# Where the rows of the moving operands stand in SBUF: from a stagger of 16 bytes to one fixed distance from the weights

## The chip, the cores and the metric

The kernel runs on one core of a Trainium2 chip. The metric is the device time of the one launch, in microseconds (us); lower is better. The same inputs are used for both kernels, and both compute the same values with the same instructions.

## The reference

Two transformer blocks follow each other, each with two layers, on 256 tokens of width 1024. Everything heavy is a matrix product of the 256 tokens with a weight matrix:

```
h = h + 0.5 * swiglu(rmsnorm(h, ffn1_norm[i]), ffn1_w_gu[i], ffn1_w_down[i])   # block 1, D_FF = 2816
u = rmsnorm(h, mix_norm[i])
... = jnp.split(u @ w_in[i], ...)            # conv branch, latent attention, two gates
h = h + merged @ w_o[i]
h = h + 0.5 * swiglu(rmsnorm(h, ffn2_norm[i]), ffn2_w_gu[i], ffn2_w_down[i])
gate = jax.nn.sigmoid(rmsnorm(h, ple_norm[i]) @ w_ple_gate[i])
h = h + gate * (p[i] @ w_ple_proj[i])

a = rmsnorm_2(h, norm_mix_pre[i])            # block 2, D_FF_2 = 4096
u = jnp.einsum('bsd,de->bse', a, w_in[i])    # sparse attention, convolution, pooling
h = h + rmsnorm_2(mix @ w_out[i], norm_mix_post[i])
m = jnp.square(jax.nn.relu(m @ w_up[i])) @ w_down[i]
h = h + rmsnorm_2(m, norm_mlp_post[i])
gate = jax.nn.sigmoid(h @ ple_gate[i])
h = h + gate * (p[i] @ ple_proj[i])
```

All of it is float32.

## The kernel before

Activations lie transposed: the 128 partitions hold 128 of the 1024 features, a row along the free dimension holds the 256 tokens (1024 bytes) of one block of features, and eight rows (k = 0 to 7) hold the whole state. Each float32 operand is split into a high part, rounded to the format `float32r`, and a low part, the rest. A product of two operands is three matmuls, weights high by x high, weights high by x low, weights low by x high, into one PSUM bank. `product` writes them, at L2028, L2029 and L2030. In nearly all of them the stationary operand is a tile of 128 x 128 of the weights, loaded anew for each matmul by a weight load (PEld), and the moving operand is a row of 256 tokens.

Weights come in chunks of 128 x 2048 (one MB) by DMA into `raw` (three buffers), ScalarE rounds a chunk into `w_hi` (L800) and VectorE subtracts it into `w_lo` (L1313), in rings of four. Within a chunk a weight tile starts at a multiple of 512 bytes.

The order of the work is written out by hand for each engine in one program of four parts (block 1 twice, block 2 twice), with semaphores between the engines. The kinds of matmuls that matter here are:

- `project`, `pair` and `halves`: eight rows of `xh` and `xl` against a chunk of weights, m = 0 and 1, 48 matmuls a chunk, into `work`. In timelines: `work<-xh,w_hi`, `work<-xl,w_hi`, `work<-xh,w_lo`. Four calls of `accumulate` in each layer of block 2 read `xh` and `xl` as well, into `acc`.
- `accumulate`: two rows of the inner tile `hh` and `hl` (in the arena `ra`) against a chunk of the down projection, 48 matmuls, into `acc`. In timelines `acc<-ra,w_hi` and `acc<-ra,w_lo`. There are 76 such chunks: 11 in each of the four feed-forward nets of block 1, 16 in each of the two of block 2. The output projection of the latent attention also goes through it, with rows `oh` and `ol`: 4 chunks in each of two layers.
- the gate: eight rows `gh` and `gl` (also in `ra`) against the gate weights, 16 chunks, 48 matmuls each.
- the projection `w_o` (`work<-ra`): eight rows `mh` and `ml` in `ra`, 8 chunks.
- by token in block 2: the rows of `xh` and `xl` are the stationary operand there, and the weights move (`work<-w_hi,xh`).

The addresses: in the built program `w_hi` starts at byte 25728 of a partition, `w_lo` at 58496, `xh` at 99456, `xl` at 107776 and `ra` at 188288. All of these but `xl` are 128 modulo 256, so counted from the weights' own address modulo 256 they are at 0, and `xl` at 128. The constant `ROW = T + 4` puts the rows of `xh`, `xl`, `hh`, `hl`, `gh` and `gl` 1040 bytes apart. So row k of `xh` and of `gh` is 16k bytes past the weights' own address modulo 256 (0 to 112), and row k of `xl` and of `gl` 128 + 16k (128 to 240). The inner tile has four rows r of each part, 16r for the high part and 64 + 16r for the low part. Below, this number is called the distance of a row. The rows `mh`, `ml`, `oh` and `ol` are 1024 bytes apart, and all of them have distance 0. In the index scores of block 2 (`dots`, `acc<-ka,ra` and `acc<-kb,ra`) the stationary operand is a tile in `ra` at 128 modulo 256 and the keys, high and low, start at 0 modulo 256 (`ka` is at byte 137984, `kb` at 144128), so there every moving row stands at distance 128 from its stationary tile.

Of the kernel before, what the change touches and what calls it, by code (L numbers as in the profile page):

```python
# [34 lines left out]
F32R = mybir.dt.float32r  # L35
# [5 lines left out]
P = 128  # L41
T = 256
TB = T // P
D = 1024
KD = D // P
# [10 lines left out]
CH = 2048  # L56
WORK = 4

ROW = T + 4
EPS = 1e-6  # L60
LN_EPS = 1e-5
NEG = -1e30
# [235 lines left out]
def build(nc, ins, out):  # L298
    with ExitStack() as ctx:
        def sb(name, shape, dt=F32):  # L300
            return ctx.enter_context(nc.sbuf_tensor(name, shape, dt))
# [6 lines left out]
        w_hi = sb("w_hi", [P, RING, CH], F32R)  # L308
        w_lo = sb("w_lo", [P, RING, CH], F32R)
        h = sb("h", [P, KD, T])  # L310
        xh = sb("xh", [P, KD, ROW], F32R)[:, :, 0:T]
        xl = sb("xl", [P, KD, ROW], F32R)[:, :, 0:T]
        consts = sb("consts", [P, C_KEPT])
        rot_r = sb("rot_r", [P, 2, P], F32R)
        zero_r = sb("zero_r", [P, P], F32R)
# [14 lines left out]
        ra = sb("ra", [P, 10240], F32R)  # L330

        def cut(arena, at, *dims):
            n = 1
            for d in dims:
                n *= d
            v = arena[:, at:at + n]
            if len(dims) == 2:
                v = v.rearrange("p (a b) -> p a b", a=dims[0])
            if len(dims) == 3:
                v = v.rearrange("p (a b c) -> p a b c", a=dims[0], b=dims[1])  # L340
            return v

        ident = consts[:, C_ID:C_ID + P]
        ones = consts[:, C_ONES:C_ONES + P]
        mask1 = consts[:, C_MASK:C_MASK + 384]
# [3 lines left out]
        lneps_col = consts[:, C_COL + 3:C_COL + 4]  # L349

        gs, si, us, hid = (cut(fa, i * 1024, 2, 2, T) for i in range(4))
        hh, hl = (cut(ra, i * 4 * ROW, 2, 2, ROW)[:, :, :, 0:T] for i in range(2))
        sq = cut(fa, 4096, KD, T)

        lat = cut(fa, 0, 6, T)
# [23 lines left out]
        krph, krpl = ra[:, 7680:7936], ra[:, 7936:8192]  # L379
        mh, ml = cut(ra, 0, KD, T), cut(ra, 2048, KD, T)  # L380

        gh, gl = (cut(ra, 4 * ROW * 4 + i * KD * ROW, KD, ROW)[:, :, 0:T] for i in range(2))

        pp = cut(fa, 0, KD, T)
        gate = cut(fa, 2048, 4, 2, T)
# [2276 lines left out]
```

## Time and profile before

| | before |
|---|---|
| median of 3 runs | 1977.84 us |
| lowest and highest | 1977.26 and 1979.76 us |
| span of the profiled execution | 1978.2 us |
| TensorE matmul busy | 1935.2 us, 98%, 16060 matmuls |
| TensorE weight load busy | 1916.9 us, 97% |
| VectorE busy | 1350.9 us, 68% |
| ScalarE busy | 996.9 us, 50% |
| GpSimd busy | 237.4 us, 12% |

No time of the profiled execution is given beside its span, 1978.2 us; the span is 0.4 us over the median of the other runs, so there is nothing around it to be added.

A matmul's own duration in the profile (280 ns) is longer than the time from its start to the next one's (about 118 ns), since matmuls are pipelined and their ends are modelled. What a matmul costs is read from starts: take the start of the first and of the one behind the last of a run of matmuls, and divide by their number. The timeline shows starts to 10 ns, so a run of 24 or 48 is exact to 0.4 ns a matmul or better, a group of three only to some 3 ns.

### The profile page before, as it was taken

The numbers are of one execution on the slowest core, as the hardware profiler recorded it, in microseconds if no ns is written. First come the engines' busy times: TensorE is split into PE (matmuls) and PEld (weight loads), VectorE is DVE, ScalarE is ACT, GpSimd is POOL, SyncE is SP. The second block draws the span as 40 slices with busy tenths as digits, with TensorE's granted clock in tenths as the row PEclk, the third lists the DMA queues.
The fourth block names the chain that finished last, engine by engine and source line by source line (L and its number), as shares of the span: only waits on it lengthen the run. The fifth ranks groups of instructions, "written<-read, shape, count | busy, mean of one in ns | idle before, by whom it ended". The sixth has DMA issues, their size and how long they took to land.

```text
span 1978.2 us, 36952 instructions
## 1 busy us (share of the span) xinstructions
PE 1935.2 (98%) x16060; PEld 1916.9 (97%) x16060; DVE 1350.9 (68%) x1608; ACT 996.9 (50%) x1233; POOL 237.4 (12%) x168
## 2 busy tenths in 40 slices
PE   8999999999999999999999999998999999899999
PEld 8999999999999999999999999898999999799998
DVE  6655777775559655687785557896855589676556
ACT  5443545563437444545554445776533466654443
POOL 3000100010002000100010001473100016710000
PEclk9999999999999999999999999999999999899999
DMA  8555454465554655544556554424555543237551
GB/s 278 199 180 182 144 174 160 133 211 192 192 183 156 213 182 183 183 137 143 171 171 213 185 181 152 158 67 132 170 187 187 166 152 113 70 112 231 191 183 53
DMA packets 246533, 329.57 MB, mean 167 GB/s; under 512 B 6246, under 2 KB 218788, under 8 KB 246372
## 3 DMA queue, kind: packets, MB, share of 16 engines
q1 hardware_dynamic: 246018, 326.79, 50.0%
q8 instruction: 127, 2.08, 0.4%
q0 software_dynamic: 96, 0.26, 0.1%
q10 hardware_dynamic: 258, 0.16, 0.0%
q14 instruction: 34, 0.28, 0.0%
HBM read 326.14 MB, written 1.05 MB: 165 GB/s over the span
## 4 chain that ended last, share of the span: by engine, by line
PE 79%; DVE 12%; POOL 3%; ACT 3%; DMA 1%; issue 1%; SPq 0%; POOLq 0%; DVEq 0%; ACTq 0%
PE work L2028 17%; PE work L2029 17%; PE work L2030 17%; PE acc L2028 9%; PE acc L2030 9%; PE acc L2029 9%; DVE w_lo L1313 4%; POOL fa L747 2%; ACT w_hi L800 1%; DVE ra L1326 1%; DMA raw<-in_w_in_dram 1%; DVE xl L1347 1%; DVE fa L1358 1%; POOL fa L741 1%; PE acc L2105 1%
## 5 line engine op out<-in xcount | busy, mean ns | idle before, releaser
L1313 DVE TENSOR_TENSOR w_lo<-raw,w_hi 128x2048 fp32r<-128x2048 f32 (+2 forms) x313 | 709.8, 2271 | 107.8 <-ACT w_hi L800 105.8
L2028 PE MATMUL work<-xh,w_hi 128*128 128x256 f32 x2560 | 721.8, 282 | 9.6 <-DVE w_lo L1313 6.1
L2029 PE MATMUL work<-xl,w_hi 128*128 128x256 f32 x2560 | 718.6, 281 | 0.0
L2030 PE MATMUL work<-xh,w_lo 128*128 128x256 f32 x2560 | 717.0, 280 | 0.0
L800 ACT ACTIVATE w_hi<-raw 128x2048 fp32r<-128x2048 f32 (+2 forms) x313 | 576.6, 1849 | 165.4 <-PE work L2030 74.6
L2028 PEld LDWEIGHTS work<-xh,w_hi 128*128 128x128 f32 x2560 | 482.3, 188 | 13.9 <-issue 8.0
L2029 PEld LDWEIGHTS work<-xl,w_hi 128*128 128x128 f32 x2560 | 483.0, 189 | 0.3
L2030 PEld LDWEIGHTS work<-xh,w_lo 128*128 128x128 f32 x2560 | 483.1, 189 | 0.0
L2028 PE MATMUL acc<-ra,w_hi 128*128 128x256 f32 x1352 | 380.1, 281 | 0.0
L2030 PE MATMUL acc<-ra,w_lo 128*128 128x256 f32 x1352 | 379.7, 281 | 0.0
L2029 PE MATMUL acc<-ra,w_hi 128*128 128x256 f32 x1352 | 378.9, 280 | 0.0
L1358 DVE TENSOR_TENSOR fa<-work,rstd 128x512 f32<-128x512 f32 x168 | 114.8, 688 | 287.1 <-PE work L2030 286.5
L2029 PEld LDWEIGHTS acc<-ra,w_hi 128*128 128x128 f32 x1352 | 255.5, 189 | 0.0
L2030 PEld LDWEIGHTS acc<-ra,w_lo 128*128 128x128 f32 x1352 | 254.8, 188 | 0.0
L2028 PEld LDWEIGHTS acc<-ra,w_hi 128*128 128x128 f32 x1352 | 254.3, 188 | 0.0
L721 POOL TENSOR_TENSOR fa<-fa 128x512 f32<-128x512 f32 x36 | 62.7, 1742 | 1457.7 <-DVE xl L1347 828.6
L2028 PE MATMUL work<-ra,w_hi 128*128 128x256 f32 x616 | 175.0, 284 | 0.6 <-DVE ra L1345 0.5
L2029 PE MATMUL work<-ra,w_hi 128*128 128x256 f32 x616 | 173.6, 282 | 0.0
L2030 PE MATMUL work<-ra,w_lo 128*128 128x256 f32 x616 | 173.6, 282 | 0.0
L2028 PEld LDWEIGHTS work<-ra,w_hi 128*128 128x128 f32 x616 | 117.1, 190 | 1.6 <-DVE ra L1345 1.4
L2029 PEld LDWEIGHTS work<-ra,w_hi 128*128 128x128 f32 x616 | 117.1, 190 | 0.1
L2030 PEld LDWEIGHTS work<-ra,w_lo 128*128 128x128 f32 x616 | 117.2, 190 | 0.0
(302 smaller groups left out, 2324.7 us busy)
## 6 DMA issues: line engine op xcount, KB each, us to landing
raw<-in_ffn_w_gu_dram SPq DMA_DIRECT2D x88, 1024.0 KB, 5.1
raw<-in_w_in_dram SPq DMA_DIRECT2D x52, 1024.0 KB, 5.5
raw<-in_ffn_w_down_dram SPq DMA_DIRECT2D x44, 1024.0 KB, 4.9
raw<-in_w_up_dram SPq DMA_DIRECT2D x32, 1024.0 KB, 5.3
raw<-in_w_down_dram SPq DMA_DIRECT2D x32, 1024.0 KB, 4.9
raw<-in_w_mla_out_dram SPq DMA_DIRECT2D x8, 1024.0 KB, 5.5
raw<-in_w_o_dram SPq DMA_DIRECT2D x8, 1024.0 KB, 4.9
raw<-in_w_ple_gate_dram SPq DMA_DIRECT2D x8, 1024.0 KB, 5.0
```

Source lines behind the costliest of these rows:

```text
L721: gp.tensor_tensor(sq[:, 0:2, :], sq[:, 0:2, :], sq[:, 2 * b:2 * b + 2, :], ALU.add).then_inc(fold_step.sem, 1)
L741: gp.tensor_tensor(taps[(j - 1) % 3], yp[:, :, j:j + T], weight, ALU.mult).then_inc(own_tap.sem, 1)
L747: last = gp.tensor_tensor(cacc, cacc, taps[(j - 1) % 3], ALU.add)
L800: act.activation(w_hi[:, s, 0:tiles * cols], raw[:, r, 0:tiles * cols], ACT.Copy).then_inc(hi_done.sem, 1)
L1313: v.tensor_tensor(w_lo[:, s, 0:n], raw[:, r, 0:n], w_hi[:, s, 0:n].bitcast(F32), ALU.subtract).then_inc(lo_done.sem, 1)
L1326: v.tensor_tensor(dst, src, hi.bitcast(F32), ALU.subtract).then_inc(unit_taken.of(unit), 1)
L1347: v.scalar_tensor_tensor(lo[:, k, :], h[:, k, :], column(here, gain + k), hi[:, k, :].bitcast(F32), ALU.mult, ALU.subtract).then_inc(xl_re ...
L1358: v.tensor_tensor(dst, bank2(unit), over(scale_row, 2), ALU.mult).then_inc(unit_taken.of(unit), 1)
L2028: pe.matmul(dst, ah, bh, start=start and i == 0, stop=False, skip_group_check=not group)
L2029: pe.matmul(dst, ah, bl, start=False, stop=False, skip_group_check=not group)
L2030: last = pe.matmul(dst, al, bh, start=False, stop=stop and i == len(pairs) - 1, skip_group_check=not group)
L2105: last = pe.matmul(dst, ones, src[:, k, :], start=k == 0, stop=k == KD - 1)
```

## The change

The constant `ROW` goes. The rows of all six tiles stand 1024 bytes apart, so all the rows of a tile have one distance, and the high and the low part of a tile have the same: 144 bytes for `xh` and `xl`, 176 for `hh` and `hl`, 208 for `gh` and `gl`. To that end `xh` and `xl` are cut out of one tensor `x_rows` of 4160 elements, the size that both had together, at elements 36 and 2084; the inner tile starts at elements 44 and 1068 of `ra`, the gate at 4212 and 6260. All other tensors keep their addresses. The instructions, their number, order, sizes, engines and semaphores are the same as before: apart from line numbers, which are 7 higher behind the edit, and the name `x_rows`, only the start addresses of operands differ.

```diff
-ROW = T + 4
+X_SIZE, X_ROW, X_AT = 4160, 256, (36, 2084)
+H_ROW, H_AT = 256, (44, 1068)
+G_ROW, G_AT = 256, (4212, 6260)
@@
-        xh = sb("xh", [P, KD, ROW], F32R)[:, :, 0:T]
-        xl = sb("xl", [P, KD, ROW], F32R)[:, :, 0:T]
+        x_rows = sb("x_rows", [P, X_SIZE], F32R)
@@
+        def rows_at(arena, at, n, row):
+
+            return cut(arena, at, n, row)[:, :, 0:T]
+
+        xh, xl = (rows_at(x_rows, at, KD, X_ROW) for at in X_AT)
@@
-        hh, hl = (cut(ra, i * 4 * ROW, 2, 2, ROW)[:, :, :, 0:T] for i in range(2))
+        hh, hl = (rows_at(ra, at, 4, H_ROW).rearrange("p (a b) t -> p a b t", a=2) for at in H_AT)
@@
-        gh, gl = (cut(ra, 4 * ROW * 4 + i * KD * ROW, KD, ROW)[:, :, 0:T] for i in range(2))
+        gh, gl = (rows_at(ra, at, KD, G_ROW) for at in G_AT)
```

## Rows read from the trace of the kernel before

**Rows 1.** The page: busy time of the engines, the clock, the chain.

```profile
PE 1935.2 (98%) x16060; PEld 1916.9 (97%) x16060; DVE 1350.9 (68%) x1608; ACT 996.9 (50%) x1233; POOL 237.4 (12%) x168
...
PEclk9999999999999999999999999999999999899999
...
PE 79%; DVE 12%; POOL 3%; ACT 3%; DMA 1%; issue 1%; SPq 0%; POOLq 0%; DVEq 0%; ACTq 0%
```

**Rows 2.** Groups by line on TensorE: count | busy us, mean ns | idle before.

```profile
L2028 PE MATMUL work<-xh,w_hi 128*128 128x256 f32 x2560 | 721.8, 282 | 9.6 <-DVE w_lo L1313 6.1 <-DVE xl L1347 1.5 <-DVE ra L1326 1.2
...
L2028 PE MATMUL acc<-ra,w_hi 128*128 128x256 f32 x1352 | 380.1, 281 | 0.0
...
L2028 PE MATMUL acc<-xh,w_hi 128*128 128x256 f32 x128 | 40.7, 318 | 1.7 <-DVE w_lo L1313 1.3 <-DVE xl L1326 0.4
```

**Rows 3.** Timeline of TensorE, one chunk of x, starts of L2028: start us, us.

```profile
99.38 0.28 PE L2028 MATMUL work<-xh,w_hi 128*128 128x256 f32 x1
...
101.50 0.28 PE L2028 MATMUL work<-xh,w_hi 128*128 128x256 f32 x1
...
101.85 0.28 PE L2028 MATMUL work<-xh,w_hi 128*128 128x256 f32 x1
...
102.19 0.28 PE L2028 MATMUL work<-xh,w_hi 128*128 128x256 f32 x1
...
104.67 0.28 PE L2028 MATMUL work<-xh,w_hi 128*128 128x256 f32 x1
...
105.02 0.28 PE L2028 MATMUL acc<-ra,w_hi 128*128 128x256 f32 x1
```

**Rows 4.** The same, the chunk of the inner tile behind it.

```profile
105.72 0.28 PE L2028 MATMUL acc<-ra,w_hi 128*128 128x256 f32 x1
...
106.06 0.28 PE L2028 MATMUL acc<-ra,w_hi 128*128 128x256 f32 x1
...
106.42 0.28 PE L2028 MATMUL acc<-ra,w_hi 128*128 128x256 f32 x1
...
106.79 0.28 PE L2028 MATMUL acc<-ra,w_hi 128*128 128x256 f32 x1
...
110.70 0.28 PE L2028 MATMUL work<-xh,w_hi 128*128 128x256 f32 x1
```

**Rows 5.** Timeline of TensorE in `w_o`, every row at distance 0.

```profile
395.25 0.28 PE L2028 MATMUL work<-ra,w_hi 128*128 128x256 f32 x1
395.37 0.28 PE L2029 MATMUL work<-ra,w_hi 128*128 128x256 f32 x1
395.49 0.28 PE L2030 MATMUL work<-ra,w_lo 128*128 128x256 f32 x1
...
398.13 0.28 PE L2028 MATMUL work<-ra,w_hi 128*128 128x256 f32 x1
...
401.01 0.28 PE L2028 MATMUL work<-ra,w_hi 128*128 128x256 f32 x1
```

**Rows 6.** Timeline of TensorE in the index scores, every key row 128 off its stationary.

```profile
1265.48 0.28 PE L2028 MATMUL acc<-ka,ra 128*128 128x256 f32 x1
...
1266.90 0.22 PE L2028 MATMUL acc<-ka,ra 128*128 128x128 f32 x1
```

**Rows 7.** Windows, TensorE alone: us, busy (matmuls), clock, DMA share, GB/s.

```profile
30.00:250.00 220.00, 220.00 (x1861) 1.00 0.54 179
```

**Rows 8.** The waits: engine line waited for: us in total, times, longest.

```profile
DVE fa L1358 <- PE work L2030: 286.5, 88, 4.9
...
ACT fa L864 <- DVE fa L1358: 155.1, 40, 4.4
...
DVE w_lo L1313 <- ACT w_hi L800: 105.8, 62, 4.1
...
ACT w_hi L800 <- PE work L2030: 74.6, 25, 3.3
```

## The prediction

> **What bounds the kernel now.** I read the page first. TensorE is busy for 1935.2 us, 98% of the span, weight loads for 97%, VectorE for 68%, ScalarE for 50%, and the clock is full in all slices but one, where it is 8 tenths [rows 1]. The chain that ended last is TensorE for 79% [rows 1]. The waits say the same from the other side: ScalarE and VectorE wait for TensorE or for each other in its shade (VectorE 286.5 us for units in `work`), while VectorE's longest kind of wait on ScalarE, 105.8 us over 62 times, lies in chunks prepared ahead [rows 8]. So the kernel is as long as its matmuls are apart, and the question is what sets the step from one start to the next.
>
> That step is what the reader is to see in the timelines. Over a whole feed-forward stretch it is 220 us / 1861 = 118.2 ns [rows 7]. In a chunk of x it is (105.02 - 99.38) / 48 = 117.5 ns [rows 3], in a chunk of the inner tile (110.70 - 105.02) / 48 = 118.3 ns [rows 3, 4]. In `w_o`, where every row has distance 0, it is 2.88 us / 24 = 120.0 ns, twice over, and each single step is 0.12 [rows 5]. Same shape, same clock, same engine, nothing waited for: only addresses differ. Within a chunk the step isn't even either. The group of three of row k = 7 of x takes 102.19 - 101.85 = 0.34 us for m = 0 and 105.02 - 104.67 = 0.35 for m = 1; the row before it takes 0.35 [rows 3]. In the inner tile one group takes 0.34 and another 0.37 [rows 4]. So the place of a row costs or saves up to 10 ns of 118. This is the whole lever of the change.
>
> A rule of the Trainium skill speaks against that. "SBUF — State Buffer", section Who interferes with whom, gives TensorE two independent read ports, one for the moving operand and one for weight loads, so that (TensorE: Matmul & The Clock Gate, section Step-by-step) loading the next tile takes no read bandwidth from the running matmul. By that rule a start address could change nothing, and the time would stay where it is. The trace disagrees: 120.0 against 117.5 ns in the same form [rows 3, 5].
>
> **The change, part by part.** No instruction is added, removed, moved or resized; no wait changes. The writers of the rows (ScalarE L816 and L870, VectorE L1347 and L1379) do the same work to other addresses; if one of them became a little slower or faster, it would lie beside a TensorE that is 98% busy, so I put that at nothing. What changes is the distance of the moving rows:
> - x: work<-x is 3 x 2560 = 7680 matmuls, acc<-x 3 x 128 = 384 [rows 2], together 8064. Row k = 1 of `xl` keeps its distance of 144; all others change.
> - inner tile: acc<-ra is 3 x 1352 = 4056 [rows 2]; 76 chunks of 48 are the inner tile, 3648.
> - gate: 16 chunks of 48, 768, at the step of x, whose layout it shares.
> - by token: 672 matmuls in which x is the stationary operand. The distance is the same thing with the operands exchanged. I give them nothing, with some 3 ns, 2 us, either way.
> The other matmuls, `w_o` among them, keep their step.
>
> So 12,480 matmuls move, and one nanosecond of step is worth 12.5 us. What the step is with all rows at one distance of 144, 176 or 208 no row shows. The bounds are the nearest rows. From below: a group of three in 0.34 us, 113.3 ns a matmul, the shortest that occurs [rows 3, 4]. Then x and gate give 4.2 x 8832 = 37 us, the inner tile 5.0 x 3648 = 18, together 55 us: 1923. From above: the step with one distance throughout that is seen longest, 120.0 ns [rows 5]: x and gate lose 2.5 x 8832 = 22 us, the inner tile 1.7 x 3648 = 6, together 28: 2006.
>
> Which value? The two places with one fixed distance are 0 (120.0) and 128, where 12 matmuls take 1266.90 - 1265.48 = 1.42 us, 118.3 ns [rows 6]. Both are special: two reads that start at one address modulo 256, or exactly half way round. The staggered rows mix sixteen distances and come out at 117.5, better than either; without 0 and 128 the other fourteen come to (16 x 117.5 - 120.0 - 118.3) / 14 = 117.3, some above and some below. The group that is fastest in its chunk, row 7, has its high and its low row at 112 and 240, neither at the start nor at the half. I take that row as the model for a fixed distance away from 0 and 128: (0.34 + 0.35) / 2 / 3 = 115.0 ns [rows 3]. Nothing but the nearest likeness picks it, and it lies in the middle between 113.3 and 117.5.
>
> The sum: x and gate 2.5 ns x 8832 = 22.1 us, inner tile 3.3 x 3648 = 12.0, together 34 us. Not all of it arrives. The chain has only 79% of TensorE against 98% busy [rows 1]: at stage ends VectorE, ScalarE and DMA set the pace, and there a faster TensorE only waits longer. I let 85% arrive, 29 us. What is late next is the preparation of weights: VectorE is busy for 1350.9 us, 32% below the span [rows 1], so it doesn't take over. The profiled span is 1978.2, 0.4 us over the median, so the forecast is 1978 - 29 = 1949 us.
>
> **The rivals.**
> - One distance is worse than many. High and low rows now meet the weight tile at one and the same place in every matmul, instead of at sixteen; if the disturbance doesn't average out, each step pays it. For it: both places with one distance are slower than the mix, 118.3 and 120.0 against 117.5 [rows 3, 5, 6]. Against it: both are the special distances. Its price by the middle of these two, 119.2 ns: x and gate 1.7 x 8832 = 15 us, inner tile 0.9 x 3648 = 3, 18 us slower: 1996; by 118.3 alone 0.8 x 8832 = 7 us: 1985. It decides once the steady step of x lies over 117.5. Losses on TensorE arrive in full. I put 1990.
> - Nothing changes: the two reads pass each other in any case, a fixed distance only shifts when, and the mean stays at 117.5 and 118.3. Against it stands the 120.0 of distance 0. 1978. This is also where the rule of the Trainium skill above would end.
> - The full gain: the three distances are free of the disturbance altogether, 113.3 ns, 55 us on TensorE, 85% of it 47: 1931.
> - The change doesn't do what it says: another tensor's address moves too. The built program excludes that; `x_rows` is as large as `xh` and `xl` were.
>
> **How the numbers follow.** Forecast 0.44, full gain 0.13, nothing 0.13, one distance worse 0.30. A measurement of this kernel can tell 0.2%, 4 us or 0.3 ns of step, from no change; so "same" is a narrow target, and the case of nothing carries it alone, with a little from the edges. Faster 0.58, same 0.13, slower 0.29. The likeliest case is 1949, its own range 1931 to 1966 (a step of 113.3 to 116.4). The range that leaves out two in ten reaches from 1922, near the lower bound if all of it arrives, to 1994, which takes in most of the slower case but not its end at 2006.
>
> **What would show it.** In the profile after, a chunk of x should take 5.52 us (48 x 115.0) from its first start to the start behind it, and all groups of three should be alike, about 0.345 us, with no slower and faster rows; a chunk of the inner tile likewise. `w_o` must stay at 2.88 us for 24, or the whole reading by distance falls. 30 to 250 us should hold about 1900 matmuls in place of 1861. VectorE's wait for `work` should shrink (286.5 us now) and that on ScalarE in `w_lo` grow. If groups still differ from each other though their distances don't, something else than the distance sets the step, and my model by row is wrong. If they are alike but over 117.5, the first rival holds. If TensorE's steps shrink and the time doesn't follow, the 85% was wrong.

## The result and the profile after: 0.6% slower

| | before | after |
|---|---|---|
| median | 1978.8 us (4 runs) | 1991.14 us (4 runs) |
| lowest and highest | 1977.26 and 1981.11 | 1988.92 and 1991.65 |
| span of the profiled execution | 1978.2 us | 1989.9 us |
| ratio, 95% interval | | 1.0058 [1.0046, 1.007] |

The forecast was 1949 us and had the wrong sign. The time came out at the rival "one distance is worse than many", priced at 1990.

The page of the kernel after, the rows that answer to [rows 1]. The lines of the program are seven higher: L2035, L2036 and L2037 were L2028, L2029 and L2030.

```profile
PE 1951.5 (98%) x16060; PEld 1933.2 (97%) x16060; DVE 1350.0 (68%) x1608; ACT 996.5 (50%) x1233; POOL 237.6 (12%) x168
...
PEclk9999999999999999999999999998999999899999
...
PE 83%; DVE 9%; POOL 3%; ACT 3%; DMA 1%; issue 1%; SPq 0%; POOLq 0%; DVEq 0%; ACTq 0%
```

TensorE is busy for 1951.5 - 1935.2 = 16.3 us more; VectorE and ScalarE are as busy as before, so the writers of the moved rows lost nothing. TensorE's share of the chain rose from 79% to 83%, and the clock stands at 8 tenths in two slices in place of one, at 9 in all others. The mean granted clock is 0.992, before it was 0.994; in the window of [rows 7] it is 1.00 in both kernels, and the matmuls are further apart there all the same. So the clock does not make the step longer there; what it adds elsewhere stands below.

The timeline of TensorE after, at the same place as [rows 3, 4]: the starts of a chunk of x, of the chunk of the inner tile behind it, and of the next chunk of x.

```profile
99.90 0.28 PE L2035 MATMUL work<-x_rows,w_hi 128*128 128x256 f32 x1
...
100.25 0.28 PE L2035 MATMUL work<-x_rows,w_hi 128*128 128x256 f32 x1
...
100.61 0.28 PE L2035 MATMUL work<-x_rows,w_hi 128*128 128x256 f32 x1
...
100.97 0.28 PE L2035 MATMUL work<-x_rows,w_hi 128*128 128x256 f32 x1
...
105.59 0.28 PE L2035 MATMUL acc<-ra,w_hi 128*128 128x256 f32 x1
...
111.32 0.28 PE L2035 MATMUL work<-x_rows,w_hi 128*128 128x256 f32 x1
```

The chunk of x takes 105.59 - 99.90 = 5.69 us, 118.5 ns a matmul, against 117.5 in [rows 3]; the inner tile 5.73 us, 119.4 ns, against 118.3 in [rows 4]. The groups of three are nearly alike, 0.35 or 0.36 us: the slow and fast rows of the stagger are gone, and what is left lies above their mean.

In `w_o`, which still has every row at distance 0, the mean is what [rows 5] showed: 24 matmuls in 2.87 and in 2.89 us, 120.0 ns.

```profile
397.03 0.28 PE L2035 MATMUL work<-ra,w_hi 128*128 128x256 f32 x1
...
399.90 0.29 PE L2035 MATMUL work<-ra,w_hi 128*128 128x256 f32 x1
...
402.79 0.28 PE L2035 MATMUL work<-ra,w_hi 128*128 128x256 f32 x1
```

The window of [rows 7] holds 1844 matmuls in place of 1861:

```profile
30.00:250.00 220.00, 220.00 (x1844) 1.00 0.54 179
```

And the waits, for [rows 8]:

```profile
DVE fa L1365 <- PE work L2037: 292.8, 87, 5.0
...
DVE w_lo L1320 <- ACT w_hi L807: 105.5, 62, 3.7
```

VectorE waits 6.3 us longer for TensorE and as long as before for ScalarE: the slower engine is TensorE.

Where the 11.7 us of span are, from the starts of all matmuls in the two traces, summed by kind of work (start to next start). The mean steps leave out those of 135 ns and more, in which something is waited for or the granted clock is at its lower level.

| | count | before, us (mean step) | after, us (mean step) | difference |
|---|---|---|---|---|
| x into `work` | 7680 | 912.7 (117.59 ns) | 919.9 (118.62 ns) | +7.2 |
| x into `acc` | 384 | 53.1 (118.12 ns) | 56.1 (118.52 ns) | +3.0, nearly all at half clock |
| inner tile and output projection into `acc` | 4056 | 480.3 (118.36 ns) | 483.9 (119.25 ns) | +3.6 |
| gate, `w_o` and the rest of `work<-ra` | 1848 | 225.3 (119.02 ns) | 225.0 (119.56 ns) | -0.3 |
| all else | | | | -1.8 |

So 10.8 of the 11.7 us lie with x into `work` and with `acc<-ra`: about one nanosecond on each of some 11,300 moved matmuls.

The 3.0 us of x into `acc` are another matter. The same twelve matmuls, the second such group of block 2, take 1.5 us before, at a granted clock of 1.00, and 2.7 us after, at 0.50 with a step of 213 ns. The window of before, then that of after:

```profile
1338.50:1340.00 1.50, 1.50 (x14) 1.00 0.00 0
```

```profile
1346.70:1349.40 2.70, 2.70 (x14) 0.50 0.00 0
```

Over the whole trace the matmuls at half clock (those to which the profile gives a length of 0.39 us or more) fill 35.8 us after and 29.9 us before, which is worth some 3 us, an estimate from these two. Whether the change causes that is not shown: executions of the kernel before alone vary in mean granted clock from 0.992 to 0.996.

Looked at step by step, without rounding, the x chunks of after show something that no view of the profile prints: the steps repeat. In x they run 115, 118, 118, 122, 121 ns and begin again, a period of five matmuls, though the program repeats every three; in the gate 119, 119, 117, 120, 124, 121, 119, 114, a period of eight. So a group of three in x takes from 351 to 361 ns, in an order that doesn't follow the rows. In `w_o`, at distance 0, every step of before is 120 after at most eight. After, the `w_o` of the first layer, the one shown, runs 117, 121, 120, 124, 118 from beginning to end, also 120.0 on the mean, though its addresses are those of before; the `w_o` of the second layer runs at 120 after eight.

### The profile page after: what moved, and what is told of

The parts are those of the page before. It is cut to its first block, busy times and chain, and to the rows that moved or that the text cites. A ratio compares the mean times of both kernels' runs of the same rounds, so it can differ in the third digit from the quotient of the medians.

```text
span 1989.9 us, 36952 instructions
## 1 busy us (share of the span) xinstructions
PE 1951.5 (98%) x16060; PEld 1933.2 (97%) x16060; DVE 1350.0 (68%) x1608; ACT 996.5 (50%) x1233; POOL 237.6 (12%) x168
## 4 chain that ended last, share of the span: by engine, by line
PE 83%; DVE 9%; POOL 3%; ACT 3%; DMA 1%; issue 1%; SPq 0%; POOLq 0%; DVEq 0%; ACTq 0%
PE work L2035 18%; PE work L2037 18%; PE work L2036 18%; PE acc L2035 9%; PE acc L2037 9%; PE acc L2036 9%; DVE w_lo L1320 3%; POOL fa L754 2%; ACT w_hi L807 1%; DMA raw<-in_w_in_dram 1%; DVE ra L1333 1%; DVE x_rows L1354 1%; PE work L2182 1%; PE acc L2112 1%; POOL fa L748 1%
## 5 line engine op out<-in xcount | busy, mean ns | idle before, releaser
L2035 PE MATMUL work<-x_rows,w_hi 128*128 128x256 f32 x2560 | 722.5, 282 | 8.8 <-DVE w_lo L1320 4.9
L2037 PE MATMUL work<-x_rows,w_lo 128*128 128x256 f32 x2560 | 717.7, 280 | 0.0
L2036 PE MATMUL work<-x_rows,w_hi 128*128 128x256 f32 x2560 | 717.7, 280 | 0.0
L807 ACT ACTIVATE w_hi<-raw 128x2048 fp32r<-128x2048 f32 (+2 forms) x313 | 576.2, 1848 | 167.7 <-PE work L2037 75.0
L2035 PEld LDWEIGHTS work<-x_rows,w_hi 128*128 128x128 f32 x2560 | 480.4, 188 | 13.4 <-issue 6.8
L2036 PEld LDWEIGHTS work<-x_rows,w_hi 128*128 128x128 f32 x2560 | 480.5, 188 | 0.3
L2037 PEld LDWEIGHTS work<-x_rows,w_lo 128*128 128x128 f32 x2560 | 480.4, 188 | 0.0
L2035 PE MATMUL acc<-ra,w_hi 128*128 128x256 f32 x1352 | 382.9, 283 | 0.0
L2037 PE MATMUL acc<-ra,w_lo 128*128 128x256 f32 x1352 | 381.4, 282 | 0.0
L2036 PE MATMUL acc<-ra,w_hi 128*128 128x256 f32 x1352 | 380.3, 281 | 0.0
L2036 PEld LDWEIGHTS acc<-ra,w_hi 128*128 128x128 f32 x1352 | 256.5, 190 | 0.0
L2037 PEld LDWEIGHTS acc<-ra,w_lo 128*128 128x128 f32 x1352 | 255.0, 189 | 0.0
L2035 PEld LDWEIGHTS acc<-ra,w_hi 128*128 128x128 f32 x1352 | 255.0, 189 | 0.0
L2035 PE MATMUL work<-ra,w_hi 128*128 128x256 f32 x616 | 175.5, 285 | 0.6 <-DVE ra L1352 0.5
L2037 PE MATMUL work<-ra,w_lo 128*128 128x256 f32 x616 | 174.1, 283 | 0.0
L2036 PE MATMUL work<-ra,w_hi 128*128 128x256 f32 x616 | 174.1, 283 | 0.0
L2035 PEld LDWEIGHTS work<-ra,w_hi 128*128 128x128 f32 x616 | 117.2, 190 | 1.5 <-DVE ra L1352 1.4
L2036 PEld LDWEIGHTS work<-ra,w_hi 128*128 128x128 f32 x616 | 117.2, 190 | 0.1
L2037 PEld LDWEIGHTS work<-ra,w_lo 128*128 128x128 f32 x616 | 117.2, 190 | 0.0
```

Source lines behind the costliest of these rows:

```text
L807: act.activation(w_hi[:, s, 0:tiles * cols], raw[:, r, 0:tiles * cols], ACT.Copy).then_inc(hi_done.sem, 1)
L2035: pe.matmul(dst, ah, bh, start=start and i == 0, stop=False, skip_group_check=not group)
L2036: pe.matmul(dst, ah, bl, start=False, stop=False, skip_group_check=not group)
L2037: last = pe.matmul(dst, al, bh, start=False, stop=stop and i == len(pairs) - 1, skip_group_check=not group)
```

## The experiments

Two theories were held against each other. One: the step at a fixed distance is a property of that distance, and only some distances are good. The other: any single distance is worse than a mix of sixteen. A third question was whether the three parts of the change add up. For every ratio below the kernel before ran on the same chip.

### One distance after another, TensorE alone

Both blocks are left out. TensorE multiplies 48 times for each case, with the triple of matmuls, the weight tiles and the shapes of the kernel, and two matmuls of 64 columns between cases. The code here and in the diffs below is shortened.

```diff
+for case in CASES:              # (distance high, distance low, row, ...)
+    mark(); mark()              # two matmuls of 64 columns
+    for m in range(2):
+        for k in range(8):      # w tiles and rows 1024 bytes apart, m = 1 starts 512 on
+            matmul(dst, w[wh], x[hi + row * k])
+            matmul(dst, w[wh], x[lo + row * k])
+            matmul(dst, w[wl], x[hi + row * k])
```

> TensorE alone: no other engine works while 42 runs of 48 matmuls (128x128 weights, 256 columns moving, a weight load for each, in groups of three as in the kernel) are issued behind each other. They differ only in where the moving rows start: one distance of 0, 16, ... 240 bytes for high and low, the staggers, distances 4 to 152 off the 16-byte grid, weights moved instead of rows, fewer columns. It leaves the two blocks out. Theory A (the addresses of the two reads alone set the step): 0 gives 120.0 ns throughout, 144 a pattern that repeats every five matmuls with mean 118.8, 176 about 119.2, 208 one of eight with mean 119.1, the stagger of x 117.6; moved weights at 112 or 144 read like distances of 144 or 112; with 128 moving columns about 112. Theory B (the other engines' reads and writes of SBUF cause part of it): steps are shorter here than in the kernel, and the order of the distances is another. Theory C (my forecast, each distance has its own step): the steps within one fixed distance are all alike.

The timeline, for four of the cases the 24th start and the 48th, 24 steps apart. These are distances 112, 144, 176 and 208.

```profile
79.81 0.28 PE L121 MATMUL ps<-x,w 128*128 128x256 f32 x1
...
82.53 0.28 PE L121 MATMUL ps<-x,w 128*128 128x256 f32 x1
...
91.59 0.28 PE L121 MATMUL ps<-x,w 128*128 128x256 f32 x1
...
94.43 0.28 PE L121 MATMUL ps<-x,w 128*128 128x256 f32 x1
...
103.37 0.28 PE L121 MATMUL ps<-x,w 128*128 128x256 f32 x1
...
106.23 0.28 PE L121 MATMUL ps<-x,w 128*128 128x256 f32 x1
...
114.98 0.29 PE L121 MATMUL ps<-x,w 128*128 128x256 f32 x1
...
117.84 0.29 PE L121 MATMUL ps<-x,w 128*128 128x256 f32 x1
```

2.72, 2.84, 2.86 and 2.86 us for 24 steps: 113.3, 118.3, 119.2 and 119.2 ns (unrounded 113.33, 118.67, 119.17 and 119.17). The same reading for all sixteen distances that are multiples of 16:

| distance | 0 | 16 | 32 | 48 | 64 | 80 | 96 | 112 |
|---|---|---|---|---|---|---|---|---|
| ns | 120.0 | 118.6 | 116.7 | 118.3 | 117.8 | 118.3 | 120.0 | 113.3 |

| distance | 128 | 144 | 160 | 176 | 192 | 208 | 224 | 240 |
|---|---|---|---|---|---|---|---|---|
| ns | 120.0 | 118.7 | 117.5 | 119.2 | 113.3 | 119.2 | 118.3 | 117.1 |

The stagger of the kernel before gives 117.6 here, its step in the kernel; 144, 176 and 208 give the steps of after (118.6, 119.4, 119.1), and 144 the same period of five. So TensorE alone makes these steps: no other engine's traffic is in them. Distance 144, measured twice, gives 118.7 and 118.8, 400 gives 118.6 and 656 gives 118.8, all three with the period of five, so there 256 bytes more change nothing. The mean over all sixteen is 117.9. Both theories get their due: eleven of the sixteen single distances are no better than the mix of the stagger, three are better by up to 0.9 ns, and two, 112 and 192, run at 113.3 ns.

Two expectations failed. Weights moved by 112 or by 144, with the rows at 0, take 120.0 ns each, where rows at the same distances, 144 and 112, take 118.7 and 113.3. And within one distance the steps are not alike, but for 0 and 128, and for 112 and 192 to a nanosecond; that they would be was the picture behind the forecast.

Other cases of the same run:
- The pair that the prediction took for its model, high rows at 112 and low rows at 240, fixed: 117.8 ns, not 115.0.
- High and low at 48 and 176: 115.5; at 0 and 128: 117.8; at 112 and 48: 119.8.
- 4 bytes off the weights: 123.3 ns, the slowest of all; 148: 121.1; 152: 120.3; 8: 117.5.
- A matmul with 64 weight columns takes 113.3 at distance 0 and at 144: half the weight tile, and the disturbance is gone at these two.
- With 128 or 192 moving columns the step is 111.7. It doesn't fall with the columns, so something else sets it; that this is the load of the next weight tile is likely but not shown.

### x alone at 144

```diff
-xh = sb("xh", [P, KD, ROW], F32R)[:, :, 0:T]
-xl = sb("xl", [P, KD, ROW], F32R)[:, :, 0:T]
+x_rows = sb("x_rows", [P, 4160], F32R)
+xh, xl = (x_rows[:, at:at + KD * 256]... for at in (36, 2084))
```

> Only the rows of x stand at the fixed distance of 144; inner tile and gate keep the stagger. Theory A (steps add up): 8064 matmuls at 118.6 ns instead of 117.6, 8 us, 0.42% slower than before, about 1987. Rival (the loss comes from the inner tile's change, and x's step is offset by waits it fills): no change, 1979.

1985.74 us against 1979.26, ratio 1.0035 [1.0022, 1.0047]: 6.5 us slower. Its x takes 921.0 us into `work` against 912.7, at 118.5 ns.

### The inner tile alone at 176

```diff
-hh, hl = (cut(ra, i * 4 * ROW, 2, 2, ROW)[:, :, :, 0:T] for i in range(2))
+hh, hl = (cut(ra, at, 2, 2, 256)[:, :, :, 0:T] for at in (44, 1068))
```

> Only the inner tile stands at the fixed distance of 176. Theory A: 3648 matmuls at 119.2 instead of 118.2 ns, 3.7 us, 0.19% slower, about 1982.5. Rival (the inner tile's matmuls are off the pace-setting path in places): under 1 us.

1981.97 us, ratio 1.0016 [1.0007, 1.0025]: 2.7 us slower. `acc<-ra` takes 484.7 us against 480.3; x keeps 117.4 ns. The two parts add up to 9.2 of the 12.3 us; what remains fits the gate and the widths of the intervals, and was not run by itself.

### x at 0

```diff
+xh, xl = (x_rows[:, at:at + KD * 256]... for at in (0, 2048))
```

> Rows of x 1024 bytes apart with distance 0, high and low, the rest as before. Theory A: 8064 matmuls at 120.0 instead of 117.6 ns, 19 us, 0.98% slower, about 1998, every step of x 120. Rival (a distance matters only through the rows' own variety): as with 144, 8 us, 1987.

1997.51 us, ratio 1.0095 [1.0081, 1.0109]: 18.2 us slower, the x steps at 119.9 ns. The window of [rows 7], which held 1861 matmuls:

```profile
30.00:250.00 220.00, 220.00 (x1832) 1.00 0.54 178
```

(119.9 - 117.6) x 8064 is 18.5 us. With the step of TensorE alone it is (120.0 - 117.6) x 8064 = 19.4. So at these two distances that step foretells the time of the kernel, to 1.2 us at 0 and to 2.4 at 144 (1.1 x 8064 = 8.9 against 6.5). The next kernel shows where this ends.

### All three at 192

```diff
+xh, xl = (x_rows[:, at:at + KD * T]... for at in (48, 2096))
+hh, hl = (cut(ra, at, 2, 2, T) for at in (48, 1072))
+gh, gl = (cut(ra, at, KD, T) for at in (4208, 6256))
```

> The change as it is, with one number other: x, inner tile and gate all at a fixed distance of 192 bytes instead of 144, 176 and 208. Theory A (each fixed distance settles into its own repeating pattern, whatever the other engines do; TensorE alone showed 113.3 ns at 192): x 4.2 ns x 8064 = 34 us, gate 3, inner tile 4.9 x 3648 = 18, 55 us less TensorE than before, and 85 to 95% of it arrives: 1927 to 1932. Rival (in the kernel VectorE and ScalarE write rows and chunks while TensorE reads, and knock it out of the fast pattern): steps near 117, 1970 or more. A step of x between says how often it is knocked out.

1973.75 us (1966.11 to 1976.17, a far wider spread than any other kernel had), ratio 0.9969 [0.9957, 0.9982]. That misses the 1927 to 1932 by over 40 us. The rival's number came true, 1970 or more with steps near 117 (x into `work` has 117.0), but not its reason. The timeline, starts of L2028 at two places:

```profile
207.63 0.28 PE L2028 MATMUL work<-x_rows,w_hi 128*128 128x256 f32 x1
...
212.93 0.28 PE L2028 MATMUL work<-x_rows,w_hi 128*128 128x256 f32 x1
...
213.53 0.47 PE L2028 MATMUL work<-x_rows,w_hi 128*128 128x256 f32 x1
...
219.19 0.28 PE L2028 MATMUL work<-x_rows,w_hi 128*128 128x256 f32 x1
...
224.63 0.28 PE L2028 MATMUL work<-x_rows,w_hi 128*128 128x256 f32 x1
```

From 207.63 to 212.93 are 15 groups, 45 matmuls: 117.8 ns each. Before 213.53 there is an interruption (a gap of 0.6 us between two starts that stand 0.34 to 0.36 apart otherwise): TensorE's own two matmuls of another kind, `acc<-fa,consts`. From 219.19 to 224.63 are 48 matmuls at 113.3 ns. The same work at the same addresses settles in either of two patterns, and keeps the one it is in until something interrupts it. Of the 94 unbroken stretches of x into `work` with 24 or more matmuls, 19 reach 113.3, within five steps, and none of these leaves it before its end; the other 75 stay in the slow one. So what decides is how TensorE comes out of an interruption, and in these stretches no write of VectorE or ScalarE knocked it out of the fast pattern.

### All three at 112

```diff
+xh, xl = (x_rows[:, at:at + KD * T]... for at in (28, 2076))
+hh, hl = (cut(ra, at, 2, 2, T) for at in (28, 1052))
+gh, gl = (cut(ra, at, KD, T) for at in (4188, 6236))
```

> The same with a fixed distance of 112. TensorE alone reached 113.3 ns there too, but only after eleven steps of about 118. Theory A: as with 192, with some ten slow steps (50 ns in all) behind each interruption; if only waits interrupt, within 5 us of the run at 192. If every change of tile restarts the search, 12 of 48 steps are slow, 1.2 ns on the mean, 15 us more than at 192.

1936.6 us (1935.73 to 1938.52), ratio 0.9788 [0.9775, 0.98]: 42.9 us less than before. The page, the timeline and the window:

```profile
PE 1890.4 (98%) x16060; PEld 1870.8 (97%) x16060; DVE 1349.8 (70%) x1608; ACT 997.9 (52%) x1233; POOL 238.8 (12%) x168
```

```profile
98.17 0.28 PE L2028 MATMUL work<-x_rows,w_hi 128*128 128x256 f32 x1
...
98.51 0.28 PE L2028 MATMUL work<-x_rows,w_hi 128*128 128x256 f32 x1
...
98.85 0.28 PE L2028 MATMUL work<-x_rows,w_hi 128*128 128x256 f32 x1
...
103.61 0.28 PE L2028 MATMUL acc<-ra,w_hi 128*128 128x256 f32 x1
```

```profile
30.00:250.00 220.00, 219.83 (x1925) 1.00 0.56 183
```

The chunk of x takes 5.44 us, 113.3 ns, every group 0.34. The step was 0.34 here and there in [rows 3]; now it is so throughout. At a distance of 112 every one of the 94 stretches of x reaches this pattern, after at most 13 steps, most of them of 116 to 121 ns. The expectation, which put this kernel level with the one at 192 or 15 us behind it, missed: it is 37 us ahead. The waits of VectorE:

```profile
DVE fa L1358 <- PE work L2030: 258.8, 85, 4.5
```

VectorE waits 27.7 us less for TensorE than in [rows 8]. The sums by kind of work fall by 25.5 us (x), 17.5 (`acc<-ra`) and 2.3 (`work<-ra`), 45.3 in all, and the span by 41.5. These sums hold waits and steps at half clock too, and both grew: the mean steps alone, times the number of matmuls (those by token, which lost 1 us, counted in), give 50.6 us, of which 82% arrived.

### Two patterns at 192, and what else is in the address

The same measurement with TensorE alone, with a switch of distance in mid-case and the weights moved too.

```diff
+if m and second: hi, lo = second, 8192 + second
+wh = (wat + k * 1024 + m * 512) // 4
```

> TensorE alone again, 38 runs of 48 matmuls; it leaves the two blocks out. Weights moved by 16 to 240 bytes with rows at 0; rows and weights moved together by 64, 128, 192 with the distance kept at 192; rows 4 and 8 bytes off 112 and 192; high and low at different distances of 192, 112 and 0; a switch from one distance to another after 24 matmuls. If the distance alone counts, moving both by the same keeps 113.3, and weights moved by 64 or 144 (distance 192 or 112) give 113.3. If the weights' own place counts, they don't: the weights moved by 144 gave 120.0 in the run before. If 192 draws in from any state and 112 doesn't, a switch to 192 gives 113.3 within a few steps, one to 112 later.

- Distance 192 as the first case gave 117.8 ns throughout; one run earlier it gave 113.3 from the third step on. Entered from 144, from 0 or from 112 in mid-case it settles at 113.3 within some six steps.
- Weights at 64 and rows at 256, again a distance of 192, stand in the list twice, as the case "weights moved by 64" and as "both moved by 64". The first time it gave 117.8, the second time 113.3: the same addresses in one run. It is the history that decides.
- Distance 112 ended at 113.3 from wherever it was entered: from 0 and from 192 after about eleven steps (up to 130 ns), from 144 after one or two.
- Weights and rows moved together by 64 and by 128, at distance 192: 113.3. By 192: 117.8, the step of the slow one of its two.
- With the rows left in place and the weights moved by 16 to 240, which gives every distance again, no case reached 113.3: moved by 144 (a distance of 112) 120.0, by 64 (a distance of 192) 117.8, the others 116.7 to 120.0. The 117.8 proves nothing, since the same addresses gave 113.3 as well. The 120.0 came in both runs of TensorE alone, in the same pattern of 119 and 121, which no case with the rows at 112 shows. So the distance alone is most likely not the whole description, and where the weights stand counts too; only two entries into that case were measured.
- 4 or 8 bytes away it is lost: 104, 108, 116 and 120 give 120.0 to 121.9, and 184, 188, 196 and 200 give 118.9 to 122.2.
- High rows at 192 and low rows at 112: 117.8; the other way round 115.6. None of the mixed pairs tried reached 113.3.
- 64 weight columns at distance 192: 119.0.

The timeline of the case that goes from distance 0 to 192, the 24th to the 31st start:

```profile
222.23 0.28 PE L119 MATMUL ps<-x,w 128*128 128x256 f32 x1
222.35 0.29 PE L117 MATMUL ps<-x,w 128*128 128x256 f32 x1
222.47 0.28 PE L118 MATMUL ps<-x,w 128*128 128x256 f32 x1
222.59 0.28 PE L119 MATMUL ps<-x,w 128*128 128x256 f32 x1
222.70 0.28 PE L117 MATMUL ps<-x,w 128*128 128x256 f32 x1
222.82 0.28 PE L118 MATMUL ps<-x,w 128*128 128x256 f32 x1
222.93 0.28 PE L119 MATMUL ps<-x,w 128*128 128x256 f32 x1
223.04 0.28 PE L117 MATMUL ps<-x,w 128*128 128x256 f32 x1
```

Steps of 0.12 turn into 0.11 within four matmuls.

The case that stands in the list twice, each time the 24th start and the 48th: 2.83 and 2.72 us for 24 steps.

```profile
62.58 0.28 PE L119 MATMUL ps<-x,w 128*128 128x256 f32 x1
...
65.41 0.28 PE L119 MATMUL ps<-x,w 128*128 128x256 f32 x1
...
133.46 0.28 PE L119 MATMUL ps<-x,w 128*128 128x256 f32 x1
...
136.18 0.28 PE L119 MATMUL ps<-x,w 128*128 128x256 f32 x1
```

### x alone at 112

```diff
+xh, xl = (x_rows[:, at:at + KD * T]... for at in (28, 2076))
```

> Only the rows of xh and xl are moved, to distance 112; inner tile, gate and the rest stay as in the kernel before. Theory (the step is set by the place alone, in any neighbourhood): the work that reads x takes 887 us instead of 913, as in the run with all three at 112, so about 25 us less than before, 1953 to 1955 us. Rival (the gain needs the other rows at 112 as well, since interruptions by other matmuls throw the pattern out and it needs some ten slow steps to come back): well under 20 us, over 1960 us.

1956.84 us, ratio 0.9884 [0.9869, 0.9899]: 22.8 us less. x into `work` takes 886.5 us, as with all three at 112 (887.2), and `acc<-ra` 480.4, as before. That is 2 us over the expected 1953 to 1955. The rival falls: the gain doesn't need its neighbours.

```profile
30.00:250.00 220.00, 220.00 (x1903) 1.00 0.56 183
```

### All at 112, with the rows that were at 0

The latent rows, the inner tiles and output rows of the attention, `mh` and `ml`, and the branch rows of block 2 move up by 28 elements too (the diff shows two lines of these); 1488 matmuls go from distance 0 to 112. To make room, `joint` moves into the end of `fa`, and `x_rows` is 128 bytes shorter. By their declared sizes the tensors from `consts` to `small` come to stand 128 bytes lower by that; the matmuls that read `consts` take as long as with the three alone.

```diff
-mh, ml = cut(ra, 0, KD, T), cut(ra, 2048, KD, T)
+mh, ml = cut(ra, 28, KD, T), cut(ra, 2076, KD, T)
-oh, ol = cut(ra, 9216, 2, T), cut(ra, 9728, 2, T)
+oh, ol = cut(ra, 9244, 2, T), cut(ra, 9756, 2, T)
```

> As the run with x, inner tile and gate at 112, and the 1488 matmuls of the arena that still read rows at distance 0 (w_o, the attention's output projection, the latent rows, the branches of block 2) are moved to 112 too. Nothing else changes in the order of the work. Theory: these steps fall from 119.9 to 113.3 ns where they stand in runs of 24 or more, 1488 x 6.6 ns = 9.8 us at most: 1927 to 1932 us against 1936.6. Rival (what is left is bound by waits for VectorE and ScalarE, so that shorter steps come back as waits): no change, 1936 us.

1930.9 us (1928.53 to 1931.84), ratio 0.9751 [0.9735, 0.9768]: 48.7 us less than before and the best of all, with an interval clear of that of the three alone. `work<-ra` takes 219.0 us, 4.0 less than with the three alone, `acc<-ra` 2.2 less, x 1.6 less.

```profile
PE 1881.0 (97%) x16060; PEld 1861.6 (96%) x16060; DVE 1351.1 (70%) x1608; ACT 997.8 (52%) x1233; POOL 237.9 (12%) x168
...
PE 79%; DVE 10%; ACT 4%; POOL 4%; issue 1%; DMA 1%; SPq 0%; POOLq 0%; DVEq 0%; ACTq 0%
```

## Why the prediction was wrong

**What held.** The bound was read rightly: the steps of TensorE set the time, and every kernel since has followed them. So was the cause, that the place of a row changes the step. The writers of the rows cost nothing, by-token work lost about half a microsecond (its step rose from 118.2 to 119.6), and `w_o` stayed at 120.0 on the mean. The mean of the fourteen fixed distances other than 0 and 128, worked out as 117.3, is 117.6 in the measurement. That 85% of a gain on TensorE arrive was close: of what the mean steps give, 82% did with all three at 112, 86% with x alone, 81% with the rest too. The lower bound of the step was real: 113.3 ns is the step of a fixed distance. With the same rows moved, all to 112, the kernel takes 1936.6 us, where the rival of the full gain had 1931.

**The step that failed** is the choice between the bounds: "I take that row as the model for a fixed distance away from 0 and 128: (0.34 + 0.35) / 2 / 3 = 115.0 ns". Three things were wrong with it.
- It read the step of row 7 as a property of row 7's distances. TensorE alone, with the rows fixed at just these distances (112 and 240), takes 117.8 ns. In the stagger a step depends on the ones ahead of it as well: the matmuls of one case of the stagger lie anywhere between 113 and 126 ns.
- It carried the value over to distances that were not its own. 144, 176 and 208 have 118.7, 119.2 and 119.2 ns. They are among the worse of the fourteen; a distance taken at random would have given about 117.6, no change.
- It treated the only two places with a fixed distance as special and set them aside. They were the only rows that showed what a fixed distance does [rows 5, 6], 120.0 and 118.3, and the changed rows came out between them. (The 118.3 itself is a short row: over 48 matmuls TensorE alone takes 120.0 ns at distance 128.) The rival took the middle, 119.2, and came out at 1996, by 118.3 at 1985; the measurement is 1991.

That the rival's 1990 is so near is in part luck. Its reason, that one distance is worse than many, holds at 144, 176 and 208; at 112 the same change gains 42.9 us.

The sum with the right steps: x 1.03 ns x 8064 = 8.3 us, inner tile 1.04 x 3648 = 3.8, gate 1.4 x 768 = 1.1, together 13; measured were 12.3. That they agree so well is luck in part: of the 11.7 us between the traces some 3 belong to the clock, so of the 13 about 9 arrived, and the rival's "losses on TensorE arrive in full" does not hold. The test that the prediction named decided as it said: the groups came out alike to the 10 ns of the timeline but over 117.5, so the first rival held. Its other sign came too: unrounded, the groups still differ by up to 10 ns at one distance, so something else than the distance of a row sets the single step, and the model by row was wrong.

The rule of the Trainium skill ("SBUF — State Buffer", Who interferes with whom) that TensorE reads its moving operand and its weights through two independent ports would have given 1978. The runs say otherwise: 113.3 to 123.3 ns for one form of matmul, and 1930.9 to 1997.5 us over nine kernels that differ in addresses alone. With half the columns in the weight tile the disturbance was gone at distances 0 and 144, though at 192 such a tile took 119.0. That the two reads meet somewhere would explain why their addresses count. That is argued, not shown: no run looks at the memory itself, and why 112 and 192 are the good ones stays open.

## What to carry to other kernels

Where a kernel's length is the step between matmuls that each load their weights, try the start addresses of the moving rows against those of the weights: all rows of the hot loops at one distance, and measure each distance on TensorE alone before building it in, entered from several others: one entry called 192 as good as 112. Take a distance that came back to its fast step from every disturbance tried (112 here), not one that only can be fast (192). Measure again when the weights themselves move. And a fast row inside a mixed sequence says nothing of how that row does by itself: the steps of a tightly packed stream depend on the ones before.

## What the runs showed of the hardware

- A stream of matmuls of 128x256 with a load of a 128x128 weight tile of `float32r` for each settles in most cases into a repeating pattern of steps, of one, three, five, eight or more matmuls, which depends on the start addresses; 256 and 512 bytes more left it the same (144, 400, 656). The levels lie at 113.3 to 120.0 ns on addresses that are multiples of 16, and up to 123.3 off them. At 2.4 GHz (the granted clock is 1.00 of it from 35 to 250 us in the first run of TensorE alone) 113.3 ns are 272 cycles and 120.0 are 288.
- One set of addresses can have two such patterns (113.3 and 117.8 ns at distance 192; at distance 0 steps of 120 throughout and a period of five, with one mean), and the last interruption decides between them. The runs of the kernel at 192 spread over 10 us, where the others spread over 2 to 5; that the two patterns make the spread is likely, but only one of its runs has a trace.
- The step is 111.7 ns with 128 and with 192 moving columns, little below the 113.3 of 256, so the columns don't set it there; the weight load is the likely cause, not shown. The Trainium skill ("TensorE: Matmul & The Clock Gate", section Back-to-back issue gap) puts a sustained stream of weight loads and matmuls at about 81 ns with 128 columns; these runs show 111.7 for this operand type.
